# Softmax attention stage of a two-block transformer kernel: another PSUM bank for the first modulation set, group sums one step earlier, two weight splits moved up

## What is computed

```python
def first_block(x, ...):
    h = rms_norm(x, g_pre_mix)
    sb_q, sb_k, sb_v, q_lat, kv_lat, k_rope = split(h @ w_in)
    o_sb = stick_breaking_attention(sb_q, sb_k, sb_v)      # 8 heads, 256 x 512
    q, k, v = latent_heads(q_lat, kv_lat, k_rope)
    o_mla = mla_attention(q, k, v)                         # causal softmax, 8 heads, 256 x 512
    mix = concatenate([rms_norm(o_sb, g_grp_sb), rms_norm(o_mla, g_grp_mla)]) @ w_o
    x = x + rms_norm(mix, g_post_mix)
    ...                                                    # conv feed-forward, gated embedding

def second_block(x, c, mod_w, mod_b, ...):
    mod = silu(c) @ mod_w + mod_b                          # 1024 x 6144, needs c only
    ...                                                    # mixer, then 32 experts of 1024 x 512
```

## Time and profile before

| | us |
|---|---|
| median of 3 runs | 992.87 |
| lowest, highest | 990.92, 993.38 |
| the profiled execution | 990.85 |
| its span | 989.0 |

### The profile page before, as it was taken

The page is one execution under the profiler, slowest core; times in us unless marked ns, Lnnn a source line. Parts: engine busy times, 40 slices in busy tenths (PEclk is TensorE's granted clock), DMA queues, the critical chain, the costliest instruction groups (busy, mean ns, idle before and its releaser), DMA issues.

```text
span 989.0 us, 12352 instructions
## 1 busy us (share of the span) xinstructions
PE 806.6 (82%) x5144; PEld 525.1 (53%) x5144; DVE 331.3 (33%) x700; ACT 309.6 (31%) x621; POOL 144.2 (15%) x153
## 2 busy tenths in 40 slices
PE   7998788999999999999979998766567665765655
PEld 5856356999997886687857542212112220221213
DVE  3324576567775554459531310001000000100001
ACT  2326365566665556645541300000100000000002
POOL 0011013345443015144400000000000000000000
PEclk9999999999999999999999999888988897789878
DMA  9923964455544565833709699999999999999995
GB/s 356 427 111 105 404 257 171 171 181 192 198 155 149 181 248 208 307 119 133 285 23 405 252 403 397 427 429 427 427 427 427 431 426 429 425 428 427 430 427 223
DMA packets 23678, 297.94 MB, mean 301 GB/s; under 512 B 2752, under 2 KB 3008, under 8 KB 5440
## 3 DMA queue, kind: packets, MB, share of 16 engines
q1 hardware_dynamic: 23616, 297.09, 74.4%
HBM read 296.03 MB, written 1.05 MB: 300 GB/s over the span
## 4 chain that ended last, share of the span: by engine, by line
PE 54%; DMA 32%; DVE 6%; ACT 5%; POOL 1%; issue 1%; SPq 0%; DVEq 0%; POOLq 0%
PE ps L186 54%; DMA ring<-in_exps 32%; ACT ar L200 1%; POOL ar L217 1%; DVE ar L206 1%; ACT yT L200 1%; ACT ar L197 1%; DVE fr L206 1%; DMA ring<-in_win 0%; DVE yT L214 0%; DVE misc L600 0%; DVE yT L206 0%; DVE rb L266 0%; DVE hT L214 0%; ACT fr L197 0%
## 5 line engine op out<-in xcount | busy, mean ns | idle before, releaser
L186 PE MATMUL ps<-ring,sq 128*32 128x512 f32 x976 | 138.6, 706 | 79.6 <-DMA ring<-in_exps 79.3
L186 PE MATMUL ps<-fr 128*128 128x256 f32 (+1 forms) x852 | 146.1, 327 | 5.9 <-DVE fr L206 4.1
L186 PE MATMUL ps<-ring,ar 128*32 128x512 f32 (+3 forms) x792 | 105.4, 621 | 47.4 <-DMA ring<-in_exps 38.7
L186 PEld LDWEIGHTS ps<-fr 128*128 128x128 f32 x852 | 126.4, 193 | 21.1 <-DVE fr L206 3.5
L186 PEld LDWEIGHTS ps<-ring,sq 128*32 128x32 f32 x976 | 29.9, 120 | 177.0 <-DMA ring<-in_exps 121.7
L186 PE MATMUL ps<-hT,ring 128*128 128x256 f32 (+2 forms) x416 | 93.3, 385 | 6.7 <-DMA ring<-in_win 6.7
L206 DVE TENSOR_TENSOR ar<-ar,ps 128x512 f32<-128x512 f32 x9 | 6.2, 688 | 257.4 <-PE ps L186 257.4
L186 PEld LDWEIGHTS ps<-hT,ring 128*128 128x128 f32 (+2 forms) x416 | 78.1, 189 | 20.7 <-DMA ring<-in_win 6.7
L186 PEld LDWEIGHTS ps<-ring,ar 128*32 128x32 f32 (+1 forms) x792 | 27.5, 120 | 108.8 <-DMA ring<-in_exps 63.4
L186 PE MATMUL ps<-ar 128*128 128x512 f32 (+9 forms) x320 | 67.2, 442 | 18.1 <-DVE ar L206 8.9
L206 DVE TENSOR_TENSOR fr<-ring,fr 128x512 fp32r<-128x512 f32 x79 | 66.2, 855 | 44.2 <-ACT fr L197 44.0
(11 more groups left out here) (194 smaller groups left out, 927.8 us busy)
## 6 DMA issues: line engine op xcount, KB each, us to landing
ring<-in_exps SPq DMA_DIRECT2D x90, 2048.0 KB, 31.0
ring<-in_modw SPq DMA_DIRECT2D x12, 2048.0 KB, 9.0
ring<-in_wup SPq DMA_DIRECT2D x11, 2048.0 KB, 10.1
ring<-in_win SPq DMA_DIRECT2D x5, 2048.0 KB, 8.8
ring<-in_wdown SPq DMA_DIRECT2D x5, 2048.0 KB, 8.2
ar<-in_exps SPq DMA_DIRECT2D x3, 2048.0 KB, 12.7
ring<-in_wo SPq DMA_DIRECT2D x2, 2048.0 KB, 9.8
ring<-in_wgate SPq DMA_DIRECT2D x2, 2048.0 KB, 8.5
```

The costliest lines, as they stand in the source:

```text
L186: return pe(lambda e: e.matmul(o, l, r, start=start, stop=stop, skip_group_check=True), *waits, inc=inc)
```

## The change

Three things are changed, all in the MLA stage.

1. The first modulation set (slots 0 to 3) accumulates in bank 5 and not in bank 4. The later sets stay in bank 4.
2. In the MLA attention's order, fill 4 (the group sums) comes ahead of step (3, 1) (the values of pair 1). The order is now a parameter; the other user of `softmax_heads` keeps the former one.
3. In fill 3, after slot 4, the loads of slots 5 and 6 and of both `w_o` chunks are put into SyncE's queue, and the pieces k = 0 and 1 of the first chunk are split at once, with VectorE's subtraction for both. In fill 6 these two pieces are left out; before, k = 0 was subtracted on GpSimd and k = 1 on VectorE.

```diff
+        mod_w = {}
+
         def mod_slot(j):
-            w = stream("modw", j)
-            s_, b = j // 4, 4
+            w = mod_w[j] if j in mod_w else stream("modw", j)
+            s_ = j // 4
+            b = 4 if s_ else 5
...
-        def softmax_heads(score_pair, mask_pair, scale, v, t_vv, bufs, small, fill=None, early=None):
+        def softmax_heads(score_pair, mask_pair, scale, v, t_vv, bufs, small, fill=None, early=None, order=((3, 1), (0, 4))):
...
-            for step, i in ((1, 0), (1, 1), (0, 0), (2, 0), (0, 1), (1, 2), (3, 0), (0, 2), (2, 1), (0, 3), (1, 3), (3, 1),
-                            (0, 4), (2, 2), (0, 5), (3, 2), (2, 3), (0, 6), (3, 3)):
+            for step, i in ((1, 0), (1, 1), (0, 0), (2, 0), (0, 1), (1, 2), (3, 0), (0, 2), (2, 1), (0, 3), (1, 3), *order,
+                            (2, 2), (0, 5), (3, 2), (2, 3), (0, 6), (3, 3)):
...
             elif i < 4:
                 mod_slot(1 + i)
+                if i == 3:
+                    mod_w.update({j: stream("modw", j) for j in (5, 6)})
+                    w_o.extend([stream("wo", j) for j in range(2)])
+                    for k in range(2):
+                        out_parts(0, k, v_tt, t_mla[0])
...
             if i == 6:
-                w_o.extend([stream("wo", j) for j in range(2)])
                 for k in range(4):
                     out_low(k, tg[k], v_tt, t_mla[0])
-                    out_parts(0, k, v_tt if k % 2 else p_tt, t_mla[0])
+                    if k > 1:
+                        out_parts(0, k, v_tt if k % 2 else p_tt, t_mla[0])
                 mod_total(0)
...
-                              ((yT[:, 0:768], yT[:, 768:1536]), (ar[:, pA:pA + 768], sq[:, 1280:2048])), small, mla_fill)):
+                              ((yT[:, 0:768], yT[:, 768:1536]), (ar[:, pA:pA + 768], sq[:, 1280:2048])), small, mla_fill,
+                              order=((0, 4), (3, 1)))):
```

## The result

| | before | changed |
|---|---|---|
| median of 17 runs each, us | 992.54 | 989.42 |
| lowest, highest | 990.92, 995.14 | 985.62, 993.31 |
| ratio, 95% interval | | 0.997, 0.9959 to 0.9981 |
| the profiled execution | 990.85, span 989.0 | 993.31, span 991.5 |

What follows compares the result with a forecast made beforehand. Bound: a chain without DMA links from 7 to 606 us, then expert loads started by TensorE's releases. Terms: 0 for bank and swap as such, -2.9 + 0.4 at the mask add, -1.3 at the splits: -3.8, 989.1 us; range 986.4 to 992.2.

Steps and rivals of the forecast that it cites:

- part 1: First modulation set in bank 5: slot 4 skips the eviction wait, so pair 3's scores end 2.9 us earlier.
- Swap: Group sums ahead of pair 1's values: root matmul input comes earlier, but the Sqrt does not; worth 0 on the chain.
- The cost of the early splits: Two VectorE subtractions ahead of pair 3's mask add take 0.4 of the 2.9 us; ScalarE's copies fit its idling.
- part 4: Missing splits at 130 us: with one GpSimd subtraction left, the projection's k=2 starts another 1.3 us earlier.
- if it takes 1.93 us again: GpSimd's remaining k=2 weight subtraction, assumed as long as the first of two before, runs from 130.57 to 132.50.
- rival (a): Full port hold: VectorE blocked for all of GpSimd's operation near 130 us; gain 3.3 us, 989.6 us; chance 0.12.
- A shift of the first expert loads unlike the one at 148 us: Sign of being wrong: first expert loads not moving like TensorE's wait at 148.40, forecast at about 144.6.
- Rival (b): Clock dips at idle places: one more, -2.1 us net, 990.8 (chance 0.11), or one less, -5.5, 987.4 (0.05).
- theory D: TensorE's clock now dips within the changed stage in many runs, eating about 1 us; cut kernel 2.8 to 3.2 us under.
- rival (c): Given back in the expert stage: DMA queue not set by releases, gain ends at 606 us; 992.9 us; chance 0.07.
- (d): The wait ahead of slot 4 stays, so only the splits' -1.3 us is left, 991.6 us; chance 0.05.
- (e): First output chunk lands late, delaying pair 3's exponentials and mask add; at 124.8 us landing, 998.0 us; chance 0.04.

Runs made afterwards that it cites:

- bank-only kernel: The kernel before with the first modulation set in bank 5 and nothing else; 989.66 us against 992.12, ratio 0.997.
- second profile: The changed kernel unaltered, run and profiled again, with an undisturbed clock in the stage; 988.07 us against 992.45, ratio 0.9959.
- last cut kernel: The changed kernel with both early subtractions behind pair 3's VectorE work and k=2 subtracted on VectorE, cut off behind the first residual; 169.34 us.
- eight reciprocals: The changed kernel with the reciprocal of the first group scale done nine times in place of once; 1001.54 us, ratio to before 1.0093.
- splits only: The kernel before with the two early weight splits only, bank 4 for all sets and the former order; 988.78 us against 992.12, ratio 0.9965.
- first profile of the changed kernel: The profiled execution of the unaltered changed kernel, slowest of its 17 runs, with low clock in 108 to 116 and 128 to 132 us; 993.31 us.
- cut changed kernel: The changed kernel cut off behind the first residual, which is written out; median 171.21 us against 176.46 for the kernel before, cut.

## Why the prediction was right

**In short.** The waits that the prediction named were the ones that bound the stage, and each part alone did there what was forecast, the splits 0.4 us more. That the median came out at 989.4, 0.3 from the forecast time, is luck in part: the stage gave 4.2 us and not 3.8, less than that reached the end (3.1 by the first medians, 3.4 by all runs), and the forecast had started from a median of before that 14 more runs lowered by 0.3.

**The bound.** The wait for the eviction held the scores of pair 3, and removing it alone gave the 2.9 us of part 1 (2.91 in the bank-only kernel).

**Swap.** Forecast 0, measured 9.75 and 27.56 us against 9.74 and 27.57 alone, and no difference in company.

**The cost of the early splits.** Forecast 0.4 us at the mask add, measured 7.25 - 6.83 = 0.42. The step "2.5 us is left" measured 9.74 - 7.25 = 2.49.

**Times of the single steps.** In the second profile the stage began 0.35 us later (mask add of pair 2 at 111.44 and not 111.09). With that taken off, the mask add of pair 3 came at 118.34 (forecast 118.3), GpSimd's operation at 130.55 (130.57), k=2 at 132.11 (132.55) and the wait ahead of k=4 at 144.22 (144.6).

**The term that was mis-sized** is part 4: 1.3 us forecast, 1.69 measured. The step that failed is "if it takes 1.93 us again". The remaining GpSimd operation took 1.48 to 1.50 us in the profiles of the changed kernel, and in the second one k=2 waited for exactly that. The upper bound of the step (1.55 us, total 4.1) was the right end. What made the first of the two operations 1.93 us long stays open; the pair took 3.63 us in all five profiles that have it. The full hold of VectorE, rival (a), cost TensorE little, but not because VectorE was free:

```profile
130.84 1.85 DVE L206 TENSOR_TENSOR fr<-hT,fr 128x256 fp32r<-128x256 f32 x2
...
131.17 1.51 DVE L206 TENSOR_TENSOR fr<-hT,fr 128x256 fp32r<-128x256 f32 x1
132.61 0.68 DVE L206 TENSOR_TENSOR fr<-ring,fr 128x512 fp32r<-128x512 f32 x1
```

These are rows of VectorE in the second profile (the second is within the first). The subtraction of tile 3 took 1.51 us beside GpSimd's 130.90 to 132.40 and ended at 132.68. In the last cut kernel, with no GpSimd operation beside it, it took 0.41. The hold came one operation earlier than I had put it. As GpSimd was done sooner, only 0.2 us of it reached k=3 (1.85 us for six matmuls in place of 1.67). The Trainium skill (SBUF — State Buffer, SBUF: two separate sides) states this hold for the whole instruction; the trace agrees for this operation.

**From the stage to the end.** The stage gained 4.2 us, the full kernel 3.4 with 0.8 to either side. I had counted the whole as carried through. The expert loads did start with the release, as forecast: the first into `ar` at 516.18 before, and in the second profile of the changed kernel at 513.33. The timelines of SyncE, before and then changed:

```profile
516.18 1.28 SPq L150 DMA_DIRECT2D ar<-in_exps  x3
```

```profile
513.33 1.28 SPq L150 DMA_DIRECT2D ar<-in_exps  x3
```

Of 4.2 - 0.35 = 3.8 us at k=4, 2.9 was left there. A shift of the first expert loads unlike the one at 148 us was named as a sign of being wrong. But between k=4 and this release the same work took 366.6 to 368.9 us over the nine full profiles, with low clocks at different places in each, so a difference of 0.9 lies within the scatter. Rival (b) is seen at work as scatter; whether it is also a rule stays open, as said under theory D. The prediction's reason for a fast changed stage, that it is denser, didn't hold in the first profile.

From the release to the end of the span it was 472.5 to 472.8 us in six of the nine, 471.1 with the eight reciprocals, 475.9 with the splits only and 476.7 in the first profile of the changed kernel. The last is why that one looked slow. Of its 3.9 us over the profile of before, 1.4 lie behind the landing of the last weights, where the clock was low. The chains, before and then changed:

```profile
942.21 30.66 DMA ring<-in_exps
972.87 0.04 issue
972.92 1.98 PE ps L186 x32
```

```profile
940.10 33.88 DMA ring<-in_exps
973.98 0.04 issue
974.03 3.21 PE ps L186 x32
```

The granted clock from 970 to 980 was 1.00 before and 0.83 in this one (0.83 too with the splits only). The other 2.5 us are lost ahead of this landing, and what costs them wasn't found.

Whether the 0.8 us between 4.2 and 3.4 is a real loss or scatter stays open, so rival (c) is excluded in whole (the gain isn't given back entirely: the ratio's interval ends at 0.9981) but not in part. The eight reciprocals, of whose 15.4 to 16.1 us some 12 to 13 arrived, speak for a part.

**Rivals (d) and (e)** didn't happen: no wait ahead of slot 4, and no DMA wait ahead of ScalarE's two copies, which began at 116.22.

## What to carry to other kernels

When a matmul group waits for the eviction of the one before it in the same PSUM bank, look at what stands behind it in TensorE's queue; if that is on the chain, another bank saves the whole wait for nothing, as long as the last reader of that bank is done in time (here at 96.80, and the first slot starts after 100). Work moved into such a gap costs what it holds back on each engine by itself: two subtractions of 0.6 us cost 0.4 us on VectorE's side and nothing on ScalarE's, and moving them behind the chain's operation gave that back. Where executions scatter by more than the effect, compare an interval between two named instructions of the stage across profiles: it repeated here to a few hundredths of a microsecond, while single executions differed by 7 us. Where it didn't repeat, the same profile showed a low clock inside the interval.

## What the runs showed of the hardware

The granted clock of the same stretch of the same program differs between executions: 0.70 in 112 to 116 us in one profile of the changed kernel, while in the other the stage had no low clock. Two of the dips shown came where TensorE had just been busy half of the time (2.00 and 2.01 of 4 us), and one made 1.59 us of scores last 2.74. But being half busy didn't always bring one: in 108 to 112 us TensorE was busy 2.02 of 4 us in the splits-only kernel too, and in the cut changed kernel, and the clock stayed at 1.00 there and in the 4 us behind. What a dip costs depends on whether TensorE is the late engine: the one at 128 us stretched a modulation slot from 1.92 to 2.94 us and the transposes from 0.88 to 1.49, of which 0.65 us reached k=4.
